# Conditioning sums of a ten-stage fp32 network on one core: four small products per group two weight chunks further on, the bias behind them

## What is computed

```python
def second_block(x, c, w_ada, b_ada, ...):
    cond = jax.nn.silu(c)
    for l in range(DEPTH):                       # 2
        mod = cond @ w_ada[l] + b_ada[l]         # (1024) @ (1024, 6144)
        sh1, sc1, g1, sh2, sc2, g2 = [m[:, None, :] for m in jnp.split(mod, 6, axis=-1)]
        h = x * (1 + sc1) + sh1
        ...
```

## Time and profile before

| | us |
|---|---|
| median of three runs | 3524.36 |
| lowest and highest run | 3523.35, 3532.81 |
| the profiled execution | 3532.7 |
| its span, first to last instruction | 3530.6 |
| TensorE busy in it | 3395.6 |
| VectorE busy in it | 1990.6 |
| ScalarE busy in it | 1337.6 |

### The profile page before, as it was taken

The page is one execution under the profiler, slowest core; times in us unless marked ns, Lnnn a source line. Parts: engine busy times, 40 slices in busy tenths (PEclk is TensorE's granted clock), DMA queues, the critical chain, the costliest instruction groups (busy, mean ns, idle before and its releaser), DMA issues.

```text
span 3530.6 us, 48359 instructions
## 1 busy us (share of the span) xinstructions
PE 3395.6 (96%) x20836; PEld 2734.4 (77%) x20836; DVE 1990.6 (56%) x2864; ACT 1337.6 (38%) x2006; POOL 4.1 (0%) x18
## 2 busy tenths in 40 slices
PE   8999986899999999999999999999999999999998
PEld 7888865778888788887588888766888887578887
DVE  5554676357554754353655434566766455866644
ACT  4332454133322433233633322254544233644433
POOL 0000000000000000000000000000000000000000
PEclk9999996699999999999999999999999999999999
DMA  5444430014444342222013223210232231013221
GB/s 191 143 143 143 136 109 21 3 66 143 145 147 144 131 140 99 96 92 84 1 66 108 96 98 126 94 54 25 84 107 96 100 139 60 31 60 108 96 96 60
DMA packets 93093, 342.49 MB, mean 97 GB/s; under 512 B 10320, under 2 KB 10960, under 8 KB 92368
## 3 DMA queue, kind: packets, MB, share of 16 engines
q1 hardware_dynamic: 92880, 339.40, 28.4%
HBM read 337.26 MB, written 2.10 MB: 96 GB/s over the span
## 4 chain that ended last, share of the span: by engine, by line
PE 85%; DVE 8%; ACT 5%; issue 1%; DMA 0%; SPq 0%; DVEq 0%; ACTq 0%
PE ps L780 20%; PE ps L781 20%; PE ps L782 20%; PE ps L816 3%; PE ps L812 3%; PE ps L813 3%; DVE SPL L2048 1%; PE ps L851 1%; PE ps L850 1%; PE ps L849 1%; ACT WK L1942 1%; PE ps L1207 1%; PE ps L835 1%; PE ps L836 1%; PE ps L837 1%
## 5 line engine op out<-in xcount | busy, mean ns | idle before, releaser
L2048 DVE TENSOR_TENSOR SPL<-RAW,SPH 128x1024 fp32r<-128x1024 f32 x522 | 635.9, 1224 | 963.4 <-ACT SPH L1452 963.3
L780 PE MATMUL ps<-HH,SPH 128*128 128x512 f32 x2332 | 921.1, 395 | 9.9 <-DVE SCR L2138 4.6
L1452 ACT ACTIVATE SPH<-RAW 128x1024 fp32r<-128x1024 f32 x522 | 547.9, 1056 | 998.5 <-PE ps L782 879.3
L781 PE MATMUL ps<-HL,SPH 128*128 128x512 f32 x2332 | 910.2, 390 | 0.0
L782 PE MATMUL ps<-HH,SPL 128*128 128x512 f32 x2332 | 910.1, 390 | 0.0
L780 PEld LDWEIGHTS ps<-HH,SPH 128*128 128x128 f32 x2332 | 438.9, 188 | 113.8 <-issue 10.7
L781 PEld LDWEIGHTS ps<-HL,SPH 128*128 128x128 f32 x2332 | 438.7, 188 | 93.5 <-issue 4.1
L782 PEld LDWEIGHTS ps<-HH,SPL 128*128 128x128 f32 x2332 | 438.8, 188 | 91.6
L780 PE MATMUL ps<-AH,SPH 128*128 128x512 f32 x1008 | 394.2, 391 | 0.0
L782 PE MATMUL ps<-AH,SPL 128*128 128x512 f32 x1008 | 392.8, 390 | 0.0
L781 PE MATMUL ps<-AL,SPH 128*128 128x512 f32 x924 | 360.0, 390 | 0.0
(11 more groups left out here) (499 smaller groups left out, 4169.5 us busy)
## 6 DMA issues: line engine op xcount, KB each, us to landing
RAW<-in_ws SPq DMA_DIRECT2D x522, 512.0 KB, 3.3
RAW<-in_wa SPq DMA_DIRECT2D x96, 512.0 KB, 3.3
WK<-in_sm SPq DMA_DIRECT2D x2, 2784.0 KB, 9.9
WK<-in_cst SPq DMA_DIRECT2D x2, 1664.0 KB, 6.7
X<-in_x SPq DMA_DIRECT2D x8, 256.0 KB, 8.0
out<-X SPq DMA_DIRECT2D x8, 256.0 KB, 2.0
WK<-in_sm SPq DMA_DIRECT2D x1, 768.0 KB, 4.8
PCT<-in_pc SPq DMA_DIRECT2D x1, 349.0 KB, 3.0
```

The source lines that it names most:

```text
L780: e.matmul(out, wh, rhs[0], start=start, stop=False)
L781: e.matmul(out, wh, rhs[1], start=False, stop=False)
L1452: e.activation(SPH[:, q:q + 1024], RAW[:, r:r + 1024], ACT.Copy).then_inc(hi_ready.did(("hi", n)))
L2048: e.tensor_tensor(SPL[:, q:q + 1024], RAW[:, r:r + 1024], SPH[:, q:q + 1024].bitcast(F32), ALU.subtract).then_inc(lo_ready.did(("lo", n)))
```

## The change

The four small products of group b stand at the begin of chunk 16b + 16 instead of 16b + 14, in the plan of the banks as in TensorE's program. The addition of the bias moves from the first to the second piece of the next group, that is from ahead of chunk 16b + 18 to ahead of chunk 16b + 20, and for the last group from 194 to 196. The number and the shapes of all instructions stay as they are.

```diff
         def plan_chunk(c):
-            if c % 16 == 14 and c < 2 * N_ADA:
-                ps.plan(("adamm", c // 16), ("mod", c // 16))
+            if c % 16 == 0 and 0 < c <= 2 * N_ADA:
+                ps.plan(("adamm", c // 16 - 1), ("mod", c // 16 - 1))
...
             def begin_chunk(c):
                 w.wait_ge(("lo", c))
-                if c % 16 == 14 and c < 2 * N_ADA:
-                    b = c // 16
+                if c % 16 == 0 and 0 < c <= 2 * N_ADA:
+                    b = c // 16 - 1
                     w.wait_ge(("adas", b), ("sel",), *ps.before("adamm", b))
...
                 w.wait_ge(("raw", item_of_ada(i)))
+                if k == 1 and b:
+                    mods(b - 1)
                 if k == 0:
-                    if b:
-                        mods(b - 1)
...
-                    if n == 2 * N_ADA + 2:
+                    if n == 2 * N_ADA + 4:
                         mods(N_ADA // 8 - 1)
```

## The result

The changed kernel took 3535.86 us, median of 20 runs (3528.07 to 3547.64), beside 3527.45 us for the kernel before (3520.28 to 3537.65, 20 runs). The ratio is 1.0024, with a 95% interval of 1.0015 to 1.0034: slower by some 8 us, and by its median within 0.3%. The forecast was +6 us, 3530.4 us in a range of 3521.5 to 3538.5, with most of the chance on "within 0.3%".

What follows compares the result with a forecast made beforehand. TensorE, busy 3395.6 of 3530.6 us, was taken to bound the kernel; -1.65 (waits) + 5.5 (bank) + 2.1 (clock) = +5.95 us, so 3524.4 + 6 = 3530.4 us, range 3521.5 to 3538.5.

Steps and rivals of the forecast that it cites:

- The wait that goes: TensorE's three waits for ADS go: group 10 in FFN3 gains 1.2 us, group 5 at MIX0's end 0.45 us.
- MIX0 swallows its 2.4 us: Group 4's 2.4 us wait inside MIX0 gains 0, since TensorE then waits for the square of line 1578 as before.
- rival that MIX0 gives its 2.4 us: VectorE's chain in MIX0 hangs on TensorE and begins 2.4 us earlier: 3528.0 us; chance 0.08.
- The bank: In FFN2 tile 6 gets tile 0's bank and must wait for its read, starting at 829.67: cost 5.5 us.
- The clock: Behind TensorE's 6.6 us stand in FFN2, about 4.3 us run at half speed: cost 2.1 us, bounds 0 and 4.8.
- The spread as a rival: The kernel's own runs lie 9.5 us apart; after's median may fall on the upper, 3538.8 us, slower; chance 0.10.

Runs made afterwards that it cites:

- group 5 alone: The kernel before with only group 5's products moved to the new place, chunk 96; ratio to before 1.0026.
- empty turns: The kernel before with one bank passed over behind the six first tiles of FFN1, FFN2 and FFN3, no instruction added; ratio to before 1.0053.
- eight products in the wait: The change plus eight unread products of constants between FFN2's sum of squares and tile 6; ratio to before 1.0009.
- reads first: VectorE reads tiles 0 and 1 ahead of its low parts: on before 1.0016, on the change 1.0030, on the change without group 5 1.0013, against before.
- reads first and chunk 6 ahead: The change with VectorE's reads of tiles 0 and 1 first, in FFN1 behind the low part of chunk 6; ratio to before 0.9981.

## Why the prediction was right, point by point

**Where the time came out.** The range held, but 3535.86 us lies above the narrower 3527 to 3534 that the forecast called its own; it was the allowance for the runs' spread that took it in. Of the 5.5 us between 3530.4 and 3535.86, 3.1 are the base (the median of before was 3524.36 in three runs and 3527.45 in twenty), and 2.4 are the effect beyond the 6 us.

**The wait that goes.** Right. No wait for ADS is left. Group 10 gave 1.25 us in FFN3 in the kernels whose FFN3 begins undisturbed (367.29 against 368.54); I had said 1.2. Group 5 gave its 0.45 us at MIX0's end: from the 5501st matmul of MIX0, the groups' own not counted, to FFN2's begin it is 48.96 us before and 48.08 after, 0.88 less, which is the wait and the 0.4 us of the products. At FFN2's begin the products then cost 0.2 us, not 0.4.

**MIX0 swallows its 2.4 us.** Right. The timeline of TensorE after, which answers to the earlier trace rows:

```profile
462.28 1.85 PE L957 MATMUL ps<-WK,CST 128*128 128x512 f32 x2 [1.98 <-DVE WK L2209]
...
468.56 2.08 PE L948 MATMUL ps<-SCR,CST 128*128 128x512 f32 x2 [4.43 <-ACT SCR L1578]
```

Counted from the stage's begin (382.14 before, 381.37 after), line 957 comes 80.91 us after it instead of 81.43, and line 948 at 87.19 instead of 87.21. The 2.38 us in front of the products have become 1.98 us in front of line 957, and line 948 comes when it came. The 0.4 us of the products behind it are swallowed too, by the wait ahead of the recurrence's first matmuls (line 984). Before and after:

```profile
535.06 3.69 PE L984 MATMUL ps<-WK 64*128 64x128 f32 x32 [4.71 <-DVE WK L2252]
```

```profile
534.35 3.60 PE L984 MATMUL ps<-WK 64*128 64x128 f32 x32 [4.75 <-DVE WK L2252]
```

That is 152.92 and 152.98 us after the stage's begin. In all thirteen profiles it is 152.9 to 153.0 or, with half clock at the stage's begin, 154.4 to 154.5 us, whether group 4 is late or not. So the rival that MIX0 gives its 2.4 us is refuted here, though not by the stage's whole length.

**The bank.** Right, and it is shown: by the kernel that differs from the change in nothing but the order of two plan calls, by group 5 alone, and by the empty turns. I had put 6.6 us of wait, it was 6.58, and the tile 5.5 us: the eight products in the wait leave 5.6 us.

**The clock.** Right in kind, and in size on average. From the first matmul of tile 6 to that of tile 7 it is 5.61 us where TensorE comes to it at full clock (eight products), and 8.19, 6.91, 8.21, 8.23 and 7.18 us behind the five idle waits of the change, of group 5 alone and of the three empty turns. That is 2.6, 1.3, 2.6, 2.6 and 1.6 us, 2.1 in the mean, the 2.1 that I took from the earlier trace rows. It differs from wait to wait and is no constant; the three waits of 6.47 us that the reads first brought into FFN1 are followed by tiles of 7.37, 7.13 and 8.27 us. The rule of the Trainium skill that I had cited (page "TensorE: Matmul & The Clock Gate", section "HAM oscillation — how this bites in real kernels"), that a stall of TensorE is followed by work at the low clock, held for all of these. It did not hold behind the waits of 1.1 us ahead of tile 7: there that tile takes 5.6 us, its time at full clock, each time.

**What I left out.** FFN2 was 9.57 us longer in the profile, and I had 7.6 for it, less what goes over from MIX0. The difference can be read at the stage's begin. The kernel after ran it at half clock in this execution, before did not; the rows of the four microseconds, after and then before:

```profile
787.00:791.00 4.00, 4.00 (x29) 3.98 (x30) 3.53 (x6) 2.82 (x5) 0.00 (x0) 0.60 0.00 0
```

```profile
789.00:793.00 4.00, 3.86 (x28) 3.73 (x29) 3.75 (x6) 2.69 (x6) 0.00 (x0) 1.00 0.00 0
```

That costs 1.3 us: against the same matmuls of before, the first is 1.99 us early, at 787.15, and the one at 792.86 only 0.65 us. In sum: from the stage's begin to the sum of squares 34.49 us against 32.93, 1.56 more, of which the rest beside the 1.3 is the small products, now this stage's; from there to tile 7 15.79 against 7.60, 8.19 more; together 9.75, and 0.18 are saved behind it, where tile 7 no longer starts out of a wait. The same happened to this profile at the begins of FFN3 and of MIX1, 1.5 us each, where before had none. In the profile of group 5 alone it didn't happen in FFN2, and that stage is 6.9 us longer. So I take these for draws at waits of 1.8 us which both kernels have. The forecast's +6 us lies within the measured interval, +5.3 to +12.0 us. Group 5 alone by itself lies as far above its forecast (1.0026 against 1.0020), while the empty turns lie below theirs. Whether the 2.5 us by which the change exceeded the sum are such draws in the mean of 20 runs or something of its own is open. One thing is worth a look: FFN3 begins at half clock in six of the seven profiles whose FFN2 has the turn behind its six tiles, and in two of the six others. If that were more than chance it would be worth some 0.8 us; thirteen profiles don't settle it.

**The spread as a rival.** I had given 0.10 to the case that the median comes out above 0.3% by the runs' own spread. The table shows where that spread is: MIX0 is from 397 to 409 us long with no order by kernel (402.7 us in the mean of the nine with group 4 late, 402.3 of the four others). Most of it falls in its recurrence of short matmuls, behind the point where all profiles agree to 1.6 us. The granted clock differs there; the rows are those of before and of the change with reads first and chunk 6 ahead:

```profile
540.00:705.00 165.00, 127.24 (x4410) 108.87 (x4396) 80.14 (x144) 46.73 (x80) 0.00 (x0) 0.68 0.02 4
```

```profile
538.00:703.00 165.00, 124.86 (x4460) 107.93 (x4460) 84.19 (x152) 51.31 (x88) 0.00 (x0) 0.76 0.02 4
```

0.68 in the one, 0.76 in the other, with MIX0 at 407.0 and 397.1 us. This is seen side by side in two profiles and wasn't made to happen.

## What to carry to other kernels

A buffer that is handed out in turn belongs to the schedule. Whoever moves the user of one turn moves the banks of all that come between, and must go through the turns where the run-ahead is wanted most; here one turn at a stage's begin, with no instruction behind it, cost 7 to 8 us, a tile of 24 matmuls and the clock behind the wait. Plan such a bank ahead of the group that needs the run-ahead, or out of the turn. And a wait that is taken away gives nothing where a later wait, whose releaser doesn't hang on the first, stands behind it: see first who is late next.

Where a result gates a whole stage, as the read of tile 0 does, it should not stand behind work that is only done ahead; but look what that work was needed for, in every stage that shares the loop.

## What the runs showed of the hardware

Eight idle waits of TensorE of 6.5 to 7.9 us were all followed by half clock (0.50 in the row above), but what it cost the tile behind them ran from 1.3 to 2.7 us. With 16 passes of work that nothing reads in such a wait, and 1.4 us of idle time left, the clock stayed at 1.00. The two waits of 2.23 us were followed by half clock, at 1.6 us each. The waits of 2.4 us in FFN1 were in three profiles and not in the four others, and the waits of 1.8 us at the begins of FFN2 and FFN3 in ten of 26, at 1.4 to 1.5 us each, with the code there the same or nearly so; those of 1.1 us ahead of tile 7 never were. So the profiles of two kernels can differ by some microseconds in a stage that nobody has touched, and a difference between two kernels should be read stage by stage over more than one pair.
